# The turns of the next pair's v, moved from ahead of a step's scores to ahead of its turns of probabilities

## The reference

```python
h = rmsnorm(x, g_norm[layer]) * (1.0 + scale[:, None, :]) + shift[:, None, :]
z = h @ w_in[layer]
q_sb, k_sb, v_sb, q_fx, k_fx, v_fx, g_path, f_logit = jnp.split(z, split_points, axis=-1)
# stick-breaking: z = q.k * scale, strictly causal
log_rem = jnp.where(causal, jax.nn.log_sigmoid(-z), 0.0)
after = lax.cumsum(log_rem, axis=3, reverse=True) - log_rem
a = jnp.where(causal, jnp.exp(jax.nn.log_sigmoid(z) + after), 0.0)
# forgetting: softmax with summed log forget gates
logits = logits + cum_q[..., :, None] - cum[..., None, :]
p = jax.nn.softmax(jnp.where(causal, logits, -jnp.inf), axis=-1)
# both
out = einsum(probabilities, v)
y = concat(rmsnorm(o_sb, g), rmsnorm(o_fx, g)) * silu(g_path)
x = x + (1.0 + gate[:, None, :]) * (y @ w_out[layer])
return rmsnorm(x, g_final)
```

## Time and profile before

| | |
|---|---|
| median of 3 runs | 714.13 us (713.03 to 714.27) |
| profiled execution | 715.86 us |
| its span | 713.5 us |
| TensorE, matmuls | 689.0 us (97%) |
| VectorE | 487.6 us (68%) |
| ScalarE | 421.6 us (59%) |
| GpSimd | 364.1 us (51%) |
| mean granted TensorE clock | 0.993 |

### The profile page before, as it was taken

The page is one execution under the profiler, slowest core; times in us unless marked ns, Lnnn a source line. Parts: engine busy times, 40 slices in busy tenths (PEclk is TensorE's granted clock), DMA queues, the critical chain, the costliest instruction groups (busy, mean ns, idle before and its releaser), DMA issues.

```text
span 713.5 us, 10800 instructions
## 1 busy us (share of the span) xinstructions
PE 689.0 (97%) x3798; PEld 579.9 (81%) x3798; DVE 487.6 (68%) x996; ACT 421.6 (59%) x879; POOL 364.1 (51%) x386
## 2 busy tenths in 40 slices
PE   6899998999999999999999999999999999999995
PEld 4667877788888888888888888888888888888884
DVE  5977996955575759555768685656686855546666
ACT  5865857775576657655766676557566755324222
POOL 1021465477984454789856546867586551312100
PEclk9999999999999999999999999999999999999999
DMA  9952222223431310334413102445032654963123
GB/s 347 410 192 89 75 102 90 63 104 119 139 127 60 118 60 1 104 119 148 140 39 118 59 1 99 154 167 177 32 121 75 223 208 166 339 221 117 61 118 119
DMA packets 35607, 93.14 MB, mean 131 GB/s; under 512 B 4441, under 2 KB 6105, under 8 KB 35042
## 3 DMA queue, kind: packets, MB, share of 16 engines
q1 hardware_dynamic: 30994, 81.05, 32.4%
q0 software_dynamic: 2832, 7.34, 3.3%
q10 hardware_dynamic: 1728, 4.06, 1.5%
HBM read 68.81 MB, written 23.63 MB: 130 GB/s over the span
## 4 chain that ended last, share of the span: by engine, by line
PE 73%; DVE 11%; POOL 6%; DMA 3%; issue 3%; ACT 3%; SPq 0%; DVEq 0%; ACTq 0%; POOLq 0%
PE psum L1688 13%; PE psum L1789 12%; PE psum L1689 12%; PE psum L1696 11%; PE psum L1777 8%; PE psum L1753 5%; PE psum L1722 4%; PE psum L1721 4%; DVE work L1309 3%; POOL work L763 2%; DMA work<-in_w_ada_t 1%; DMA work<-in_x 1%; POOL w_lo L711 1%; DVE stacks L1274 1%; DVE v_stack_early L1214 1%
## 5 line engine op out<-in xcount | busy, mean ns | idle before, releaser
L1688 PE MATMUL psum<-h_hi,w_hi 128*128 128x512 f32 x448 | 185.0, 413 | 0.3
L1689 PE MATMUL psum<-h_lo,w_hi 128*128 128x512 f32 x448 | 176.4, 394 | 0.0
L1008 ACT ACTIVATE pt_hi<-psum 128x512 fp32r<-128x512 f32 (+1 forms) x192 | 87.4, 490 | 69.8 <-PE psum L1753 67.3
L1370 DVE TENSOR_TENSOR pt_lo<-psum,pt_hi 128x512 fp32r<-128x512 f32 (+1 forms) x192 | 100.5, 551 | 39.9 <-ACT pt_hi L1008 38.5
L763 POOL TENSOR_TENSOR work<-work 128x127 f32<-128x127 f32 (+3 forms) x64 | 83.7, 1308 | 79.0 <-DVE work L1309 79.0
L1696 PE MATMUL psum<-h_hi,w_lo 128*128 128x512 f32 x448 | 120.4, 390 | 0.0
L1309 DVE TENSOR_TENSOR_SCAN work<-work,eye 128x128 f32<-128x128 f32 (+3 forms) x64 | 101.4, 1585 | 24.1 <-ACT work L969 23.7
L1696 PEld LDWEIGHTS psum<-h_hi,w_lo 128*128 128x128 f32 x448 | 84.2, 188 | 18.9
L1688 PEld LDWEIGHTS psum<-h_hi,w_hi 128*128 128x128 f32 x448 | 84.5, 189 | 15.3 <-issue 0.6
L1689 PEld LDWEIGHTS psum<-h_lo,w_hi 128*128 128x128 f32 x448 | 84.8, 189 | 14.7
L769 POOL TENSOR_SCALAR work<-work,small 128x128 f32<-128x128 f32 (+3 forms) x64 | 48.0, 751 | 93.0 <-DVE small L1332 92.8
(11 more groups left out here) (201 smaller groups left out, 1320.8 us busy)
## 6 DMA issues: line engine op xcount, KB each, us to landing
w_raw<-in_w_blocks SPq DMA_DIRECT2D x30, 512.0 KB, 4.1
w_split_scratch<-work SPq DMA_DIRECT2D x16, 512.0 KB, 3.0
work<-in_x SPq DMA_DIRECT2D x12, 512.0 KB, 7.1
y_split_scratch<-work SPq DMA_DIRECT2D x10, 512.0 KB, 3.6
work<-in_w_ada_t SPq DMA_DIRECT2D x8, 512.0 KB, 10.7
v_stack_early<-in_w_ada_t SPq DMA_DIRECT2D x8, 512.0 KB, 3.3
work<-forget_scratch SPq DMA_DIRECT2D x8, 512.0 KB, 5.8
work<-in_w_out SPq DMA_DIRECT2D x16, 256.0 KB, 3.2
```

The costliest lines, as they stand in the source:

```text
L1008: nc.scalar.activation(pt_hi[:, a:e, (g % 2) * P:(g % 2 + 1) * P], bank, ACT.Copy).then_inc(s_thi, 1)
L1370: nc.vector.tensor_tensor(pt_lo[:, a:e, q0:q0 + P], bank, pt_hi[:, a:e, q0:q0 + P].bitcast(fp32), ALU.subtract).then_inc(s_tfree, 1)
L1688: nc.tensor.matmul(bank, hi, h_hi[:, c_, cols], start=(c_ == 0), stop=False)
L1689: nc.tensor.matmul(bank, hi, h_lo[:, c_, cols], start=False, stop=False)
```

## The change

In TensorE's program the call of transpose_v moves from ahead of scores to behind scores and values, directly ahead of transpose_probs. It applies to steps 9 and 10 of pairs 0 to 6, and to step 2 of pair 0: 15 runs of four turns. No other engine's program changes, nor the numbering of the runs of turns.

```diff
@@ -1850,10 +1850,6 @@
                         sb_part(n)
                 if p == LAST and i in (SUMS_AT, SUMS_AT + 1):
                     sum_squares(p - 1 if i == SUMS_AT else p - 2)
-                if i in V_NEXT and p + 1 < PAIRS:
-                    transpose_v(p + 1, V_NEXT.index(i))
-                if g == V_FIRST:
-                    transpose_v(0, 1)
                 if g + 2 < UNITS:
                     scores(g + 2)
                 if g % 2 == 0 and g >= 2:
@@ -1861,6 +1857,10 @@
                 if (p, i) == (LAST, SB_FROM):
                     for n in SB_AT[i]:
                         sb_part(n)
+                if i in V_NEXT and p + 1 < PAIRS:
+                    transpose_v(p + 1, V_NEXT.index(i))
+                if g == V_FIRST:
+                    transpose_v(0, 1)
                 transpose_probs(g)
                 if g == 0:
                     proj(u, 0, DC // 2)
```

## The result

The changed kernel took 720.92 us (719.13 to 722.32, 4 runs) against 714.2 us: ratio 1.0092, 95% interval 1.0069 to 1.0114, so 6.6 us slower (4.9 to 8.1). A second series of the same kernel gave 1.0082 (1.0061 to 1.0103), 5.9 us. The forecast was 719.6, 5.5 us slower than before.

A forecast was written before the change was run, and what follows sets the result against it. TensorE's matmul rate was taken as the bound. Forgetting pairs 3.0, stick-breaking pairs 1.9 and pair 0 0.9, less TensorE's gain of 0.3, make 5.5 us on the median 714.13: 719.6 us, range 716.4 to 721.2.

The forecast's parts named there:

- The reading that TensorE's matmul rate is the bound and only near-late work counts: Middle of the kernel: TensorE, busy 689.0 of 713.5 us, sets the pace; other engines matter only where one is late.
- two named waits: TensorE waiting for k's bank (L1274) in step 12 of odd pairs, and for the score bank (L969) in step 11 of even.
- Forgetting pairs, 1.00 us each: Pairs 1, 3, 5: step 10's later turns delay VectorE's L1274, so TensorE's projection of step 12 loses 1.00 us; 3.0 in all.
- Stick-breaking pairs, 0.62 us each: Pairs 2, 4, 6: ScalarE's L969 frees the score bank late, so TensorE loses about 0.62 us in step 11; 1.9 in all.
- Pair 0, 0.26 and 0.64 us: Pair 0: 0.26 us lost through VectorE from step 2, nothing in step 9, 0.64 from step 10; together 0.9 us.
- TensorE's own gain, 0.02 us a run: TensorE's 15 runs of turns: adjacent runs share a boundary, mostly offset by narrow matmuls ahead; 0.3 us gained in all.
- The sum, 5.5 us: Whole kernel: 3.0 + 1.9 + 0.9 - 0.3 = 5.5 us slower, 719.6 on the median.
- The hidden chain: Steps 11 and 12: the late evictions are absorbed by slack, leaving TensorE's gain and pair 0's loss; +0.6, 714.7 us; 10%.
- the half case: Pairs 1 to 6: only one of the two mechanisms holds, or later slack gives some back; 716.6 to 717.7 us; 14%.
- The faster case: Pair 0's stall at 116.68: turns ahead of it keep the clock at 2.4 GHz, saving 1.6 us; 711.9 us; 3%.
- The second clock drop: Pairs 1, 3, 5: the new idle 0.9 us halves TensorE's clock, 1.6 us more per pair; 724.4 us; 8%.
- What I said would be unchanged: Sign to look for in the trace after: pair 7 and the end of the kernel stay unchanged.

The follow-up runs named there:

- these pairs alone: Against the kernel before, only v's turns in step 10 of pairs 1, 3 and 5 moved behind scores and values; 717.7 us, ratio 1.0042.
- L1274 first: On the changed kernel, VectorE takes k's first half (L1274) out ahead of the scores in step 10 of the odd pairs too; 722.82 us, ratio 1.0114.
- pair 0 alone: Against the kernel before, only pair 0's three runs of v's turns (steps 2, 9 and 10) moved; 715.54 us, ratio 1.0011.
- the parts alone: Four kernels, each the kernel before with one part moved: step 10 of odd pairs, of even pairs, step 9, pair 0; 3.0 + 1.6 + 0.2 + 0.8 us.
- the kernel with no turn moved: Kernel before, TensorE's program untouched; ScalarE and VectorE take the output's eviction (values_out) ahead of v's (vt_out); 719.16 us, ratio 1.0066.
- the kernel with the even pairs alone: Against the kernel before, only v's turns in step 10 of pairs 2, 4 and 6 moved; 716.19 us, ratio 1.0023.
- the one with the output first after the move: On the changed kernel, ScalarE and VectorE take the output's eviction (values_out) ahead of v's (vt_out); 717.87 us, ratio 1.0047.
- the one with the turns last: On the kernel before, v's turns go behind the turns of probabilities, and vt_out to the step's end on ScalarE and VectorE; 718.89 us, ratio 1.0063.

## Why the prediction was right, point by point

- **The reading that TensorE's matmul rate is the bound and only near-late work counts** held: every microsecond lost in pairs 1 to 5 stands behind one of two named waits.
- **Forgetting pairs, 1.00 us each**: measured 0.98 to 1.02 in two profiles of after and 1.00 to 1.02 with these pairs alone; in time 3.0 us against 3.0. The decisive reading was that the place had no slack (0.46 us where the same turns take 0.35). The later kernel with L1274 first confirmed it: there the distance fell to 0.35.
- **Stick-breaking pairs, 0.62 us each**: 0.68 or 0.69 in step 11 of after, of which 0.06 to 0.11 make up for a gain in steps 9 and 10, and 0.65 alone. In time 1.6 against 1.9.
- **Pair 0, 0.26 and 0.64 us**: 0.30 and 0.67 in the profile with pair 0 alone. In time 0.8 against 0.9, though its interval takes in zero. The first half came as forecast there and in the first profile of after; the second profile of after has 0.49. The second has the size by luck: I had followed VectorE's lateness to L1777 in step 12, and TensorE met ScalarE's L969 at the score bank in step 11 first. The sum also held for the half clock that the profile of before has there. Where the clock stays up, kernels that leave pair 0 alone lose 0.3 us in step 12 that the moved ones don't, so step 10's move costs about 0.3 us less in those executions.
- **TensorE's own gain, 0.02 us a run**: 0.03 to 0.05 us in an odd pair and 0.06 to 0.11 us in an even one for its two runs, half a microsecond at most. The term was small and about right. The rule of the Trainium skill ("TensorE: Matmul & The Clock Gate", the part on engine queue depths) on weight loads pulled ahead would, by my estimate, have made it a loss of 1.6 us; no profile shows that.
- **The sum, 5.5 us**: the parts alone add up to 5.6, the whole was measured at 6.6 and 5.9. The intervals hold 5.5 and don't say that anything is missing. The mean granted clock of an execution differs within one kernel, from 0.991 to 0.997 in before and from 0.989 to 0.997 in after. At the same mean clock the two kernels stand 5.0 us apart (0.997: 718.8 and 713.8), 5.2 us (0.992) and 5.5 us (0.991), with two or three executions of after in each and more than one chip. So part of the 6.6 us is likely the clock of that series. I can't show an effect of the parts together; none was found in the second profile of after.
- **Rivals.** The hidden chain and the half case are out, since each of the two mechanisms showed alone. The faster case rested on the stall of step 9; it took 1.79 us in before and 1.43 and 1.72 us in the two profiles of after, of which the first kept the clock and the second lost it. So one kernel does both. The terms of that case don't add up to its 711.9 us: they give 712.4 with pair 0's 0.9 us and 711.5 without. Nothing hangs on it. The second clock drop did not come: after 0.93 us without a matmul at 198.44 the granted clock is 1.00 from 198.40 to 203.00.
- **What I said would be unchanged**, pair 7 and the end, was 1.6 us longer in both profiles of after. That is the stretch at half clock described below, and the kernel with no turn moved has it too.

## What to carry to other kernels

An engine that runs in a fixed order has places where it waits anyway, and work in such a place is free, as v's eviction was here. What a move on one engine costs is read on the engines that follow it: take the new lateness, subtract their idle gaps one by one, and look at who waits at the end of the chain. Follow every engine that passes the lateness on, and not only the slowest: in pair 0 the one I had not followed got there first. A buffer whose next user starts right behind its release (0.12 us here) is a bound even on a busy engine: compare the same group of instructions at a place where nothing can make it wait. And a wait taken away by a swap turns up at whoever was put behind (here 1.6 us for 1.0), so price the one that moves back with the full length of what passes it.

## What the runs showed of the hardware that I had not expected

TensorE's clock fell to half while its matmul row was full. In pair 7, where the transfers' share is at 1, TensorE runs two groups of 16 matmuls of one column each (L1762), some scores and turns between them. After:

```profile
589.94 1.84 PE L1762 MATMUL psum<-ones,sq_sum 128*128 128x1 f32 x16
...
592.83 2.68 PE L1762 MATMUL psum<-ones,sq_sum 128*128 128x1 f32 x16
...
594.00:595.50 1.50, 1.50 (x9) 1.50 (x8) 1.45 (x6) 1.49 (x3) 0.00 (x0) 0.50 1.08 401
595.50:597.00 1.50, 1.50 (x5) 1.01 (x4) 1.41 (x2) 1.48 (x3) 0.00 (x0) 0.50 1.03 404
```

(In the windows clock, DMA share and GB/s are the last three columns, as in the earlier trace rows.) The clock stood at 1.00 (2.4 GHz) up to 593.76, inside the second group, and then at 0.50 (1.2 GHz) for 6.8 us. In before it fell at 591.18, at the end of the second group, and for 3.4 us. In ten of twelve profiles it fell inside the second group or at most 0.2 us behind its end; in the kernel with the even pairs alone and in the one with the output first after the move it did not, with the same two groups and the same load:

```profile
590.30 1.91 PE L1762 MATMUL psum<-ones,sq_sum 128*128 128x1 f32 x16
...
594.00:595.50 1.50, 1.50 (x9) 1.24 (x9) 0.45 (x1) 1.47 (x3) 0.00 (x0) 1.00 1.03 412
```

So a full matmul row does not say that the clock is safe. Whether the one-column matmuls or the transfers have a part in it no run here shows, since both stand there in all twelve. The change may have a part in the length: it was 6.8 us in the six profiles whose pair 7 starts 1.4 us or more later than in before, 3.4 us in the four at most 0.2 us later, and the two without a fall lie between. No run tests this, and the spread of the mean clock within each kernel speaks against a fixed tie.

Nor does the length of the stall in pair 0's step 9 decide alone whether the clock falls behind it: it fell after 1.79 us without a matmul in before, 1.73 and 1.72 us in two others, and stayed up after 1.78 us in the kernel with k first and 1.97 us in the one with the turns last. The Trainium skill ("TensorE: Matmul & The Clock Gate", the section on the clock gate's warm-up) says that activity is judged on a time grid that runs freely; that would fit equal stalls with different ends, and no run here shows it.

What the clock costs is read from the steps. Half clock in pair 0 makes step 10 1.6 us longer. The stretch of 6.8 us makes pair 7 1.6 us longer than the one of 3.4 us; the two profiles without any saved 1.6 us of that in step 4 and then lost 1.3 us in step 5, where the turns waited 1.1 us for VectorE, so they ended only 0.3 us ahead of before. Together that can move one execution by some 3 us, more than most of the parts measured here (the executions of before lie between 712.85 and 716.76 us), so only many executions of each kernel tell the parts apart.
